# Eight conditioning rows move from the second mixer to the dense layer, and TensorE's loop gets a hint

## The reference, cut to what matters

```python
c_act = jax.nn.silu(c)
for l in range(DEPTH):                                   # DEPTH = 2
    mod = (c_act @ w_mod[l] + b_mod[l])[:, None, :]      # w_mod (2, 1024, 6144)
    sh1, sc1, g1, sh2, sc2, g2 = jnp.split(mod, 6, axis=-1)
    h = x * (1.0 + sc1) + sh1
    y = hybrid_mixer(h, w_in[l], w_a2[l], b_a[l], gla_norm_g[l], w_out[l])
    x = layer_norm(DN_ALPHA * x + (1.0 + g1) * y, ln_g[l, 0], ln_b[l, 0])
    h = x * (1.0 + sc2) + sh2
    y = swiglu(...) if l % 2 == 0 else moe_swiglu(...)   # D_FF = 2816, 8 experts, top 2
    x = layer_norm(DN_ALPHA * x + (1.0 + g2) * y, ln_g[l, 1], ln_b[l, 1])
```

## Time and profile before

| | us |
|---|---|
| profiled execution, whole time | 1338.73 |
| its span | 1337.0 |
| PE busy, share of the span | 1212.0, 91% |
| DVE busy | 555.3, 42% |
| ACT busy | 317.8, 24% |
| mean granted TensorE clock | 0.968 |
| chain that ended last: PE, DVE, DMA, issue | 71%, 16%, 6%, 3% |

### The profile page before, as it was taken

How to read it: one execution, slowest core, us unless ns; L and a number is a source line. 1 busy time by engine, 2 the same in 40 slices (tenths; PEclk the granted TensorE clock), 3 DMA queues, 4 the chain that set the end, 5 groups by cost and what they waited for, 6 DMA issues and landing times.

```text
span 1337.0 us, 26405 instructions
## 1 busy us (share of the span) xinstructions
PE 1212.0 (91%) x11264; PEld 657.1 (49%) x11264; DVE 555.3 (42%) x846; ACT 317.8 (24%) x552; POOL 43.3 (3%) x86
## 2 busy tenths in 40 slices
PE   2888879899978896899999999999999999999992
PEld 1888867788858885433334233333233333333331
DVE  6898886777668996420020110210210210200206
ACT  0656142344236551220011100201200200200202
POOL 2100010000010001000000000000000000000001
PEclk9999989999989998899999999999999999999996
DMA  9954778799518459579989979989889999999820
GB/s 341 308 190 159 268 256 288 283 385 319 173 50 275 160 187 403 195 287 413 413 328 404 367 268 411 405 333 387 325 330 412 367 370 375 348 404 413 327 118 31
DMA packets 149084, 403.62 MB, mean 302 GB/s; under 512 B 19964, under 2 KB 71328, under 8 KB 137696
## 3 DMA queue, kind: packets, MB, share of 16 engines
q1 hardware_dynamic: 146720, 395.16, 78.9%
q0 software_dynamic: 2240, 6.68, 1.4%
HBM read 400.75 MB, written 1.05 MB: 301 GB/s over the span
## 4 chain that ended last, share of the span: by engine, by line
PE 71%; DVE 16%; DMA 6%; issue 3%; ACT 2%; SPq 1%; POOL 0%; DVEq 0%; POOLq 0%; ACTq 0%
PE bank L1275 34%; PE bank L1299 17%; PE bank L325 4%; PE bank L327 4%; PE bank L326 4%; DVE u_low L1486 2%; DVE mod_acc L1475 2%; DMA raw_u<-in_ffn_w_up_dram 2%; DMA u_raw<-in_w_in_dram 2%; PE bank L1309 2%; PE bank L1255 1%; DMA mod_first<-in_w_mod_dram 1%; PE bank L975 1%; PE bank L1280 1%; PE bank L1178 1%
## 5 line engine op out<-in xcount | busy, mean ns | idle before, releaser
L1275 PE MATMUL bank<-raw_w,xg 128*32 128x512 f32 x4096 | 460.8, 596 | 5.6 <-issue 5.5
L1275 PEld LDWEIGHTS bank<-raw_w,xg 128*32 128x32 f32 x4096 | 127.1, 110 | 267.4 <-issue 265.3
L1299 PE MATMUL bank<-raw_w,heT 128*32 128x512 f32 x2112 | 232.9, 593 | 0.6 <-ACT heT L848 0.6
L1837 DVE TENSOR_TENSOR he<-he,bank 128x256 f32<-128x256 f32 x64 | 23.4, 417 | 384.2 <-ACT he L837 384.2
L1299 PEld LDWEIGHTS bank<-raw_w,heT 128*32 128x32 f32 x2112 | 66.9, 110 | 149.4 <-issue 147.5
L837 ACT ACTIVATE he<-bank 128x256 f32<-128x256 f32 (+1 forms) x72 | 21.4, 370 | 414.9 <-PE bank L1275 284.0
L1864 DVE SCALAR_TENSOR_TENSOR ycat<-bank,gate_tab,ycat 128x512 f32<-128x512 f32 x36 | 25.5, 747 | 191.9 <-PE bank L1264 191.9
L1475 DVE SCALAR_TENSOR_TENSOR mod_acc<-mod_row,c_act,mod_acc 128x1024 f32<-128x1024 f32 x70 | 89.9, 1285 | 9.4 <-DMA mod_row<-in_w_mod_dram 3.8
L325 PE MATMUL bank<-u_high,hT_H 128*128 128x256 f32 x256 | 75.0, 293 | 4.6 <-DVE u_low L1486 4.6
L327 PE MATMUL bank<-u_high,hT_L 128*128 128x256 f32 x256 | 72.9, 285 | 0.0
L326 PE MATMUL bank<-u_low,hT_H 128*128 128x256 f32 x256 | 72.7, 284 | 0.0
(11 more groups left out here) (278 smaller groups left out, 1499.0 us busy)
## 6 DMA issues: line engine op xcount, KB each, us to landing
raw_w<-in_moe_w_down_dram SPq DMA_DIRECT2D x88, 1024.0 KB, 8.4
raw_w<-in_moe_w_gate_dram SPq DMA_DIRECT2D x128, 512.0 KB, 7.3
raw_w<-in_moe_w_up_dram SPq DMA_DIRECT2D x128, 512.0 KB, 8.7
mod_row<-in_w_mod_dram SPq DMA_DIRECT2D x80, 512.0 KB, 6.5
raw_w<-in_moe_w_gate_dram SPq DMA_DIRECT2D x64, 384.0 KB, 3.7
raw_w<-in_moe_w_up_dram SPq DMA_DIRECT2D x64, 384.0 KB, 4.8
u_raw<-in_w_in_dram SPq DMA_DIRECT2D x20, 1024.0 KB, 7.1
raw_d<-in_ffn_w_down_dram SPq DMA_DIRECT2D x11, 1024.0 KB, 10.0
```

The source lines that it names most:

```text
L1275: last = mm(bank[m // 4][32 * q:32 * q + 32, :].rearrange("s (m f) -> s m f", m=2), xg[:, i, k, 32 * g:32 * g + 32], W[:, :, a * 256:(a + ...
L1299: last = mm(bank[3 + g][32 * q:32 * q + 32, :], heT[:, i, at:at + 32], W[:, b, h * 512:(h + 1) * 512], start=(c == 0 and a == 0), stop=(c ...
L1837: last = V.tensor_tensor(he[:, b, :], he[:, b, :], bank[b][:, 256:512], ALU.mult)
```

## The change

Vector 10 moves whole: the dense layer takes rows 24 to 71, six in each of its steps 1 to 3 and five in each of steps 4 to 9, where it took five in steps 1 to 4 and four in steps 5 to 9. Mixer 1 takes rows 72 to 79 in the places where it took 64 to 71. The column sums of vectors 5 to 8 come one step earlier. TensorE's loop over the expert pairs is opened with `hint_back_edge=True`: each pass then begins with an instruction that names the target of the loop's closing branch ahead of time.

```diff
-ROWS_DENSE, ROWS_MIX1 = 24, 64
-ROWS_AT_STEP = (0, 5, 5, 5, 5, 4, 4, 4, 4, 4, 0)
-MOD_AT_STEP = {3: 5, 5: 6, 6: 7, 8: 8}
+ROWS_DENSE, ROWS_MIX1 = 24, 72
+ROWS_AT_STEP = (0, 6, 6, 6, 5, 5, 5, 5, 5, 5, 0)
+MOD_AT_STEP = {2: 5, 4: 6, 5: 7, 7: 8}
...
-           + (HF + YC) * 10
-           + YC + HF + YC + HF + HF + [X0 + i for i in range(4)] + HF)
+           + (HF + YC) * 12
+           + YC + HF + YC + HF)
...
-                               {5: (64, 65), 8: (66, 67), 9: (68, 69), 14: (70, 71), 15: (72, 73)})
+                               {5: (72, 73), 8: (74, 75), 9: (76, 77), 14: (78, 79)})
...
-            load_mod_rows(*range(74, len(MOD_ROWS)))
...
-                    pe.wait_ge(s["row_rd"], ROWS_MIX1)
+                    pe.wait_ge(s["row_rd"], 64)
                     gate_sum(9, (0, 1))
...
-            with pe.Fori(0, n_last) as pr:
+            with nc.Fori(0, n_last, engines=[pe.engine], hint_back_edge=True) as pr:
...
-                condition_rows(range(64, 66) if l else range(4, 6))
+                condition_rows(range(72, 74) if l else range(4, 6))
...
-                condition_rows(range(66, 72) if l else range(6, 12))
+                condition_rows(range(74, 80) if l else range(6, 12))
...
-                condition_rows(range(72, 76) if l else range(12, 16))
+                if l == 0:
+                    condition_rows(range(12, 16))
                 gate_apply(10 if l else 2, (1, 2), g_row)
                 low_unit(l, NIN + 3)
-                condition_rows(range(76, 80) if l else range(16, 24))
                 if l == 0:
+                    condition_rows(range(16, 24))
```

More of the change, by code:

```diff
@@ L387, in load_mod_rows @@
                         sp.wait_ge(s["mod_ps"], 1)
-                    if n in (6, 66):
+                    if n in (6, 74):
                         sp.wait_ge(s["proj"], mix * NU + U_KEYS + 1)
[L390 to L393, removed]
+                    if n == 12:
+                        sp.wait_ge(s["pv_ps"], 2)
+                    if n == 14:
+                        sp.wait_ge(s["yT_L"], 4)
                     if n == ROWS_DENSE:
@@ L772, in mixer @@
                 evacuate(l, U_BG1)
-                act.wait_ge(s["row_rd"], 72 if l else 12)
+                act.wait_ge(s["row_rd"], 80 if l else 12)
                 for g in range(2, NG):
```

## The result

The change makes the kernel slower: 1349.28 us (1346.41 to 1356.60, eight runs) against 1341.43 (eight runs of the kernel before), a ratio of 1.0065 with a 95% interval of 1.0046 to 1.0084: 0.65% slower, a small effect but clear of the noise. The forecast was 1339.0, and its range ended at 1346. The profiled execution has a span of 1346.9 us, 9.9 more than before.

What follows compares the result with a forecast made beforehand. TensorE, busy 91% of the span, was taken to bound the kernel, with SP's load order bounding five-row dense steps. Dense +7.9, mixer 1 -1.2 and hint -8.2 gave -1.5 us: 1339.0, range 1334 to 1346.

Steps and rivals of the forecast that it cites:

- What bounds the dense layer: Dense layer: next weights queue on SP behind a fifth row waiting for DVE's first; this loop sets 18.55 us per five-row step.
- The failing step: Dense layer, six-row steps: the added row loads were given no bandwidth cost, 0 us, in loops of 19.93 us.
- The sixth row's wait: Dense steps 1 to 3: the sixth row waits for the second, adding 1.38 us to the loop, 19.93 in all.
- the forecast 59.4: Dense layer, three six-row steps: first rows 19.55, 19.93 and 19.93 us apart.
- Slow landings: Dense layer: weights landing late once in four steps before; one kept at 2.1 us, with bounds of none and three.
- The fall of the clock: Dense step 4: TensorE's clock falls after its wait, as it did before, costing 1.75 us.
- Mixer 1: End of mixer 1: without the last four rows TensorE no longer waits ahead of the last gate sum, -1.2 us.
- The hint: Expert loop: naming the branch target early removes idle and low clock at two taken branches, 8.2 of 8.55 us saved.
- Rival (b): Expert loop: the hint does nothing, so the dense loop decides; +6.7 us, 1347.2; chance 0.19.
- rival (c): Expert loop: the hint helps the taken branches but the exit pays 4.3 us; 1343.3; chance 0.10.
- The small stretches: Outside the three priced parts: dense step 1's first row stays at 204.85, earlier expert loads gain 0.
- the dense term: Dense layer: taking 48 rows costs +7.9 us, 5.8 plus one slow landing of 2.1; bounds 1.8 and 12.1.

Runs made afterwards that it cites:

- e4: The changed kernel with the fifth row's load in each six-row dense step cut to 128 of its 1024 columns; 1346.5 us, ratio 1.0024.
- e10: The changed kernel with every dense row that waits for a row of its own step loaded with 128 of 1024 columns; 1333.32 us, ratio 0.9949.
- e8: The kernel before (40 dense rows) with the hint and SP issuing gate and up weights ahead of the waiting rows; 1326.26 us, ratio 0.9893.
- e9: The changed kernel (48 dense rows, hint) with SP issuing gate and up weights ahead of the waiting rows; 1326.36 us, ratio 0.9895.
- e11: e9 with the six rows behind the logits in mixer 1 loaded and summed at the mixer's end; 1321.34 us, ratio 0.9853.

## Why the prediction was wrong

- **What bounds the dense layer: right.** The loop through SP's order, the fifth row's wait, its 18.5 us, and that the change would close it where four rows had left it open all showed. The five-row steps took 18.76, 18.72 and 18.79 where 18.55 stood.
- **The failing step** is this one: "The row loads come out of the same queue, but the 19.93 us hold 6 MB and rows 6 shows room (DMA share 0.79 to 0.85), so I add nothing for bandwidth". A mean share says nothing about a landing that is waited for: in the three slow steps it was 0.83, 0.77 and 0.79, no higher. The sixth row's wait was priced (1.38 us), its 512 KB ahead of the weights were not: landings of 10.9 to 11.7 instead of 9.0, so three steps took 66.5 us instead of the forecast 59.4, +7.1. Small rows take it back: 61.9 with one of the two (e4), 57.6 with both (e10). With one full row's landing added, 57.6 + 3 x 1.1 = 60.9 by my estimate, so some 5.6 of the 7.1 are the second row's bytes. The rest lies mainly in the second step, whose landing of 9.16 in e10 isn't explained.
- **Slow landings.** One of 2.1 us was kept, and two slow steps came, 7 (20.74 us) and 8 (19.93), 2.2 and 1.4 over 18.55. The fall of the clock that I counted into step 4 (19.41 us) did not come there (18.76, clock 1.00). With 0.2 us more in steps 5 and 6, the five-row steps came to 96.9 us instead of 95.7. A slow step is not only a slow landing. In step 7 the issue of the gate weights took 1.64 us where it takes 0.43, and the landing 0.8 more; in the kernel before, step 3, the issue took 1.08 and the landing 1.4 more.

```profile
330.38 1.64 SPq L441 DMA_DIRECT2D raw_g<-in_ffn_w_gate_dram  x1
```

In the eleven traces nine such issues took 0.80 to 1.64 us. At each of the nine a packet of the "instruction" queue starts, between 0.52 us ahead of the issue's start and 0.02 behind it (here at 330.40); the others took 0.63 at most, and none of them has one there. No run changes this, so it is not shown that SP waits for its own instructions there. In e10 the landings of steps 7 and 8 are as short as the others (8.15, 8.04), and the late issues (1.38 and 1.00 us) remain with the longer periods. Why step 8 of the changed kernel, issued in 0.43 us, lands late isn't settled.
- Together the first rows are 163.4 us apart from step 1 to 9, not 155.1: the dense layer cost 16.2 instead of 7.9.
- **Mixer 1: right in size** (-1.4 for -1.2). e8 and e9 say more than I did: where no loop is closed, the whole move is worth nothing that the times can show.
- **The hint: right** (-7.6 to -7.9 for -8.2). Rival (b) fell, and rival (c), a price at the exit, too. The Trainium skill (Runtime: NRT & Kernel Launch, section on instruction fetch mechanics) calls prefetch purely sequential. For a hinted branch these traces don't bear that out: 0.12 to 0.46 us stand where 2.7 to 3.2 stood.
- The small stretches that I had at nothing came to +1.1, +0.8 and +0.8, as much as traces of one code differ.

The signs of all parts were right, and "slower" came from the dense term, which was half its size for want of the price of the second row's bytes.

## What to carry to other kernels

Read a DMA queue as an instruction stream: a load that waits for a buffer delays all that is queued behind it, so issue what other engines need soonest ahead of the loads that wait, and early enough that most of it has landed when these go out. When a load is put ahead of another on which a loop turns, add its bytes to the landing, however much room the mean share shows. Before moving work off a stage, find its instructions on the chain: eight rows from the idle end of mixer 1 were worth nothing, six from its middle, moved to that end, some 4 us.

## What the runs showed of the hardware that I had not expected

A short wait costs more than its length where the clock falls behind it, and small shifts decide on that. In e9 TensorE waits 1.95 us for the attention output just ahead of the gate sum, and the granted clock of the stretch is 0.76; the four matmuls of the gate sum take 3.46 us. In e11 the wait isn't there, the clock is 1.00, and the same four take 1.88. The length of a wait doesn't decide it alone: in the changed kernel the matmul behind the waits of 3.39 and 1.87 us takes 0.76 and 0.62 us, the one behind 3.45 us takes 0.47.

```profile
484.49 1.25 PE L1043 MATMUL bank<-ident,ycat 128*128 128x128 f32 x8 [1.95 <-DVE ycat L1620]
485.54 3.46 PE L941 MATMUL bank<-mod_acc,ones 128*128 128x512 f32 x4
```
```profile
482.87 2.21 PE L1043 MATMUL bank<-ident,ycat 128*128 128x128 f32 x16
484.93 1.88 PE L941 MATMUL bank<-mod_acc,ones 128*128 128x512 f32 x4
```
